# Channels in fours of neighbours: a new order of the model dimension through a two-layer transformer step, with 16 KB runs of expert weights

## The reference

```
aff = softmax(h @ w_router)                  # 640 x 16
gsel, idx = top_k(aff.T, C)                  # C = 64 latent + 16 context tokens per expert
xs = h[idx]                                  # 80 rows of 1024 channels
hid = silu(xs @ w_gate[e]) * (xs @ w_up[e])  # both weights 1024 x 1024
y += scatter(hid @ w_down[e] * gsel, idx)    # 1024 x 1024
```

## Time and profile before

| | us |
|---|---|
| three runs: median (lowest to highest) | 1780.83 (1779.23 to 1781.92) |
| profiled execution: its own time | 1777.96 |
| its span | 1776.2 |
| TensorE matmul busy / weight load busy | 1626.3 / 1275.9 |
| VectorE / ScalarE / GpSimd busy | 815.0 / 581.9 / 393.5 |

### The profile page before, as it was taken

How to read it: one execution, slowest core, us unless ns; L and a number is a source line. 1 busy time by engine, 2 the same in 40 slices (tenths; PEclk the granted TensorE clock), 3 DMA queues, 4 the chain that set the end, 5 groups by cost and what they waited for, 6 DMA issues and landing times.

```text
span 1776.2 us, 71059 instructions
## 1 busy us (share of the span) xinstructions
PE 1626.3 (92%) x27949; PEld 1275.9 (72%) x27949; DVE 815.0 (46%) x2574; ACT 581.9 (33%) x2311; POOL 393.5 (22%) x2167
## 2 busy tenths in 40 slices
PE   6999989988999999998869999999889998999994
PEld 3554457447999989988745454764489998998884
DVE  2199867153323333232344996843623232333233
ACT  2200157335545432221130002753445544121211
POOL 2100000002343424342310000000124333343332
PEclk9999999999999999999979999999999999999997
DMA  9446740238999999999963412321599999999993
GB/s 342 143 163 245 256 177 1 107 115 308 397 409 410 409 410 410 409 410 410 403 223 136 171 60 74 141 95 36 225 383 409 410 410 409 409 410 410 409 410 143
DMA packets 146646, 502.07 MB, mean 283 GB/s; under 512 B 6211, under 2 KB 6628, under 8 KB 146566
## 3 DMA queue, kind: packets, MB, share of 16 engines
q1 hardware_dynamic: 142276, 488.96, 70.8%
q0 software_dynamic: 3264, 10.88, 1.9%
q10 hardware_dynamic: 1026, 1.25, 0.2%
HBM read 494.76 MB, written 6.31 MB: 282 GB/s over the span
## 4 chain that ended last, share of the span: by engine, by line
PE 63%; DMA 25%; DVE 7%; ACT 2%; issue 2%; DVEq 0%; POOL 0%; POOLq 0%; ACTq 0%; SPq 0%
PE ps L957 18%; PE ps L702 15%; DMA weight_ring<-in_w_down_dram 11%; PE ps L974 9%; DMA weight_ring<-in_w_up_dram 8%; PE ps L840 7%; DMA weight_ring<-in_w_gate_dram 5%; PE ps L736 4%; PE ps L581 2%; DVE neg_m L1559 2%; PE ps L784 1%; PE ps L646 1%; ACT weight_ring L1151 1%; DMA qk<-in_x_sample_dram 1%; PE ps L894 1%
## 5 line engine op out<-in xcount | busy, mean ns | idle before, releaser
L957 PE MATMUL ps<-v_sb,weight_ring 128*64 128x80 f32 x16384 | 583.1, 233 | 29.5 <-DMA weight_ring<-in_w_gate_dram 14.4
L957 PEld LDWEIGHTS ps<-v_sb,weight_ring 128*64 128x64 f32 x16384 | 571.2, 137 | 41.2 <-DMA weight_ring<-in_w_gate_dram 18.2
L974 PE MATMUL ps<-v_sb,weight_ring 128*64 128x80 f32 x8192 | 295.0, 233 | 34.4 <-DVE v_sb L1720 21.6
L974 PEld LDWEIGHTS ps<-v_sb,weight_ring 128*64 128x64 f32 x8192 | 286.7, 137 | 42.7 <-DVE v_sb L1720 26.8
L702 PE MATMUL ps<-mix,weight_ring 128*128 128x128 f32 (+1 forms) x976 | 271.3, 439 | 2.1 <-ACT mix L1061 1.2
L1254 ACT ACTIVATE v_sb<-mix 128x8 f32 x1520 | 183.0, 204 | 228.8 <-PE ps L957 144.5
L1746 DVE TENSOR_TENSOR qk<-qk,v_sb 128x8 f32 x1520 | 210.9, 193 | 98.4 <-issue 95.8
L1880 POOL COPY v_sb<-mix 128x8 f32 x1040 | 145.4, 200 | 459.7 <-PE ps L957 396.0
L1893 POOL TENSOR_TENSOR qk<-qk,v_sb 128x8 f32 x1040 | 201.0, 237 | 178.1 <-DVE v_sb L1735 173.9
L702 PEld LDWEIGHTS ps<-mix,weight_ring 128*128 128x128 f32 x976 | 148.0, 194 | 123.2 <-issue 120.3
L1471 DVE SCALAR_TENSOR_TENSOR weight_ring<-u_gate,conv_cols,weight_ring 128x655 f32<-128x655 f32 x240 | 195.3, 893 | 0.0
(11 more groups left out here) (201 smaller groups left out, 1265.8 us busy)
## 6 DMA issues: line engine op xcount, KB each, us to landing
weight_ring<-in_w_down_dram SPq DMA_DIRECT2D x64, 2048.0 KB, 22.3
weight_ring<-in_w_gate_dram SPq DMA_DIRECT2D x48, 2048.0 KB, 19.5
weight_ring<-in_w_up_dram SPq DMA_DIRECT2D x48, 2048.0 KB, 23.0
weight_ring<-in_w_mod_dram SPq DMA_DIRECT2D x24, 2048.0 KB, 8.4
weight_ring<-in_w_in_dram SPq DMA_DIRECT2D x10, 2048.0 KB, 8.9
spare<-in_w_gate_dram SPq DMA_DIRECT2D x32, 512.0 KB, 10.7
weight_ring<-in_w_out_dram SPq DMA_DIRECT2D x4, 2048.0 KB, 9.5
rope_sb<-in_w_gate_dram SPq DMA_DIRECT2D x16, 512.0 KB, 11.5
```

The source lines that it names most:

```text
L957: last = nc.tensor.matmul(ps[c * HALF:(c + 1) * HALF, 2 * (i % 2) + f // BLK, f % BLK * CAP:(f % BLK + 1) * CAP], w[:, kk, o:o + HALF], pi ...
L974: last = nc.tensor.matmul(ps[c * HALF:(c + 1) * HALF, 4 + d // BLK, d % BLK * CAP:(d % BLK + 1) * CAP], w[:, kk, o:o + HALF], hid[:, k, :] ...
```

## The change

The channel order of the residual stream, and the hidden order in an expert, becomes: channel 512b + 4p + j lies on partition p, in chunk 4b + j (RUN = 4). `run_rows` reads a weight in that order, and the four rows that one partition needs of half a matrix are neighbours in memory. `in_run` is the matching slice of 128 (or 64) columns with a step of 4 elements.

1. `expert_unit`: one contiguous run of 16 KB per partition where four of 4 KB were. A relay piece remains 4 KB per partition.
2. The stationary slices in `gate_up` and `down` have a step of 4 elements (16 bytes).
3. `transpose_x`, `x2_transposes` and `modulation_cols` read with that step; `transpose_back` and the gate transposes write PSUM with it.
4. `proj_unit` issues four DMAs of 512 KB where it issued one of 2 MB (2 KB rows as before); `load_router` issues four.
5. The bias and gain rows are loaded as 512-wide rows and transposed with four strided slices per layer, beside one for the rest.
6. In units 0 and 1 TensorE goes through kk outermost and signals (`pieces_used`) after each of the first three quarters. ScalarE copies piece j as soon as quarter j was used, and the last when the unit was.

```diff
+RUN = 4
+        pieces_used = [signal(f"pieces_used{r}", (RELAY - 1) * EXPERTS) for r in range(RELAYS)]
+        def run_rows(w):
+            return w.rearrange("(b p j) n -> p b j n", p=P, j=RUN)
+        def in_run(k, p0=0, n=P):
+            first = k // RUN * RUN * P + k % RUN + RUN * p0
+            return slice(first, first + RUN * (n - 1) + 1, RUN)
...
+                for j in range(RUN):
+                    sp.dma_start(dst[:, :, j, :], src[:, :, j, :]).then_inc(proj_loaded[i % 2].sem, 16)
...
-                return w[l, e].rearrange("(k p) n -> p k n", p=P)[:, half * 4:half * 4 + 4, :]
+                return run_rows(w[l, e])[:, half:half + 1]
...
-                sp.dma_start(relay[r][j], expert_src(l, e, r)[:, j, :]).then_inc(relay_loaded[r].sem, 16)
+                sp.dma_start(relay[r][j], expert_rows(l, e, r)[:, j // RUN, j % RUN, :]).then_inc(relay_loaded[r].sem, 16)
...
-                sp.dma_start(ring[:, UNIT_SLOTS[l][i], :].rearrange("p (k n) -> p k n", k=KD // 2), expert_src(l, e, i))\
-                  .then_inc(expert_loaded[i].sem, 16)
+                sp.dma_start(ring[:, UNIT_SLOTS[l][i], :].rearrange("p (b n) -> p b n", b=1),
+                             expert_rows(l, e, i).rearrange("p b j n -> p b (j n)")).then_inc(expert_loaded[i].sem, 16)
...
-                    last = nc.tensor.transpose(ps[:, 2 * (t % 3) + k // 4, tokens(k % 4)], x2_t[:, k, tokens(t)], ident[:])
+                    last = nc.tensor.transpose(ps[:, 2 * (t % 3) + k // 4, in_run(k % 4)], x2_t[:, k, tokens(t)], ident[:])
...
-                                               x_all[:, t, tokens(k)], ident[:])
+                                               x_all[:, t, in_run(k)], ident[:])
...
+                        order = [(f, kk) for f in range(KD) for kk in range(KD // 2)]
+                        if i < RELAYS:
+                            order.sort(key=lambda at: at[1])
+                        for f, kk in order:
...
-                                        w[:, kk, o:o + HALF], picked_t[:, k, :],
+                                    w[:, kk, in_run(f, c * HALF, HALF)], picked_t[:, k, :],
...
+                            if i < RELAYS and f == KD - 1 and kk < RELAY - 1:
+                                last.then_inc(pieces_used[i].sem, 1)
...
                 def relay_copy(e, r):
-                    act.wait_ge(*expert_used.at(l, (e - 1) * 6 + r + 1))
                     act.wait_ge(*relay_loaded[r].at(l, e * RELAY))
-                    w = ring[:, UNIT_SLOTS[l][r], :].rearrange("p (j n) -> p j n", j=RELAY)
                     for j in range(RELAY - 1):
+                        act.wait_ge(*pieces_used[r].at(l, (e - 1) * (RELAY - 1) + j + 1))
                         nc.scalar.activation(w[:, j, :], relay[r][j], ACT.Copy).then_inc(relay_copied[r].sem, 1)
+                    act.wait_ge(*expert_used.at(l, (e - 1) * 6 + r + 1))
```

More of the change, by code:

```diff
@@ L165, in build @@
         conv_rows = free_slots[0:TAPS * CH, P:P + DEPTH * P].rearrange("p (l n) -> p l n", l=DEPTH)
-        par_rows = free_slots[0:C_ALL, 3 * P:3 * P + DEPTH * P].rearrange("p (l n) -> p l n", l=DEPTH)
+        chan_rows = free_slots[0:C_CB // RUN, 3 * P:3 * P + DEPTH * RUN * P].rearrange("p (l n) -> p l n", l=DEPTH)
+        par_rows = free_slots[0:C_ALL - C_CB, 12 * P:12 * P + DEPTH * P].rearrange("p (l n) -> p l n", l=DEPTH)
         past_k = x_norm[:, 0:DEPTH * BANK].rearrange("p (l n) -> p l n", l=DEPTH)
@@ L218, in build @@
         past_copied = signal("past_copied")
-        proj_loaded = [signal(f"proj_loaded{b}", 3 - b, 16) for b in range(2)]
+        proj_loaded = [signal(f"proj_loaded{b}", 3 - b, 16 * RUN) for b in range(2)]
         mod_loaded = [signal(f"mod_loaded{s}", unit=16) for s in range(SLOTS)]
@@ L293, in build @@
         h2_hi_ready = signal("h2_hi_ready", TILES)
-        router_loaded = signal("router_loaded", 1, 16)
+        router_loaded = signal("router_loaded", 1, 16 * RUN)
         strips_done = signal("strips_done", TILES)
@@ L416, in proj_unit @@
             def proj_unit(l, i):
-                sp.dma_start(ring[:, PROJ_SLOTS[l][i % 2], :].rearrange("p (k n) -> p k n", k=KD),
-                             rows8(w_in[l])[:, :, PROJ_ORDER[i] * BANK:(PROJ_ORDER[i] + 1) * BANK])\
-                  .then_inc(proj_loaded[i % 2].sem, 16)
+                dst = ring[:, PROJ_SLOTS[l][i % 2], :].rearrange("p (b j n) -> p b j n", j=RUN, n=BANK)
+                src = run_rows(w_in[l])[:, :, :, PROJ_ORDER[i] * BANK:(PROJ_ORDER[i] + 1) * BANK]
+                for j in range(RUN):
+                    sp.dma_start(dst[:, :, j, :], src[:, :, j, :]).then_inc(proj_loaded[i % 2].sem, 16)
             def mod_unit(l, u):
@@ L429, in out_unit, with expert_rows @@
                              rows8(w_out[l])[:, half * 4:half * 4 + 4, :]).then_inc(out_loaded[half].sem, 16)
-            def expert_src(l, e, i):
+            def expert_rows(l, e, i):
                 w, half = (w_gate, w_up)[i % 2] if i < 4 else w_down, i // 2 if i < 4 else i - 4
-                return w[l, e].rearrange("(k p) n -> p k n", p=P)[:, half * 4:half * 4 + 4, :]
+                return run_rows(w[l, e])[:, half:half + 1]
             def relay_piece(l, e, r, j):
-                sp.dma_start(relay[r][j], expert_src(l, e, r)[:, j, :]).then_inc(relay_loaded[r].sem, 16)
+                sp.dma_start(relay[r][j], expert_rows(l, e, r)[:, j // RUN, j % RUN, :]).then_inc(relay_loaded[r].sem, 16)
             def expert_unit(l, e, i):
-                sp.dma_start(ring[:, UNIT_SLOTS[l][i], :].rearrange("p (k n) -> p k n", k=KD // 2), expert_src(l, e, i))\
-                  .then_inc(expert_loaded[i].sem, 16)
+                sp.dma_start(ring[:, UNIT_SLOTS[l][i], :].rearrange("p (b n) -> p b n", b=1),
+                             expert_rows(l, e, i).rearrange("p b j n -> p b (j n)")).then_inc(expert_loaded[i].sem, 16)
             sp.dma_start(cond_rows[0:KD, :], c_ctx.rearrange("(k p) -> k p", p=P)).then_inc(cond_loaded.sem, 16)
@@ L545, in _ @@
                 o = PAR_COL + l * C_ALL
-                last = nc.tensor.transpose(ps[:, 7, o:o + C_ALL], par_rows[:, l, :], ident[0:C_ALL, 0:C_ALL])
+                for j in range(RUN):
+                    nc.tensor.transpose(ps[:, 7, o + j:o + C_CB - RUN + j + 1:RUN], chan_rows[:, l, in_run(j)],
+                                        ident[0:C_CB // RUN, 0:C_CB // RUN])
+                last = nc.tensor.transpose(ps[:, 7, o + C_CB:o + C_ALL], par_rows[:, l, :],
+                                           ident[0:C_ALL - C_CB, 0:C_ALL - C_CB])
             last.then_inc(setup_transposed.sem, 1)
@@ L590, in modulation_cols @@
                     col = MOD_COLS * (mod_region(l, group) * BLK + b)
-                    last = nc.tensor.matmul(ps[:, 7, col:col + MOD_COLS], mod_rows[:, tokens(b)], pair_sum,
+                    last = nc.tensor.matmul(ps[:, 7, col:col + MOD_COLS], mod_rows[:, in_run(b)], pair_sum,
                                             start=True, stop=True)
@@ L852, in x2_transposes @@
                     for k in range(KD):
-                        last = nc.tensor.transpose(ps[:, 4 + k // 4, tokens(k % 4)], x_tile[:, i % 2, tokens(k)], ident[:])
+                        last = nc.tensor.transpose(ps[:, 4 + k // 4, tokens(k % 4)], x_tile[:, i % 2, in_run(k)], ident[:])
                     last.then_inc(x2_transposed.sem, 1)
@@ L900, in _ @@
                         g = mod[:, l, 2 * KD + k, v:v + 1].to_broadcast([P, P])
-                        last = nc.tensor.transpose(ps[:, 2 + 2 * v + k // 4, tokens(k % 4)], g, ident[:])
+                        last = nc.tensor.transpose(ps[:, 2 + 2 * v + k // 4, in_run(k % 4)], g, ident[:])
                 last.then_inc(gates_transposed.sem, 1)
@@ L951, in gate_up @@
                         w = ring[:, UNIT_SLOTS[l][i], :].rearrange("p (k n) -> p k n", k=KD // 2)
[L952 to L959, removed]
-                                        w[:, kk, o:o + HALF], picked_t[:, k, :],
-                                        start=(k == 0 and f % BLK == 0), stop=(k == KD - 1 and f % BLK == BLK - 1))
+                        order = [(f, kk) for f in range(KD) for kk in range(KD // 2)]
+                        if i < RELAYS:
+                            order.sort(key=lambda at: at[1])
+                        for f, kk in order:
+                            k = (i // 2) * (KD // 2) + kk
+                            for c in range(2):
+                                last = nc.tensor.matmul(
+                                    ps[c * HALF:(c + 1) * HALF, 2 * (i % 2) + f // BLK,
+                                       f % BLK * CAP:(f % BLK + 1) * CAP],
+                                    w[:, kk, in_run(f, c * HALF, HALF)], picked_t[:, k, :],
+                                    start=(k == 0 and f % BLK == 0), stop=(k == KD - 1 and f % BLK == BLK - 1))
+                            if i < RELAYS and f == KD - 1 and kk < RELAY - 1:
```

(27 more changed lines are left out.)

## The result

The changed kernel takes 2349.2 us (median of 4 runs, 2348.29 to 2350.07) against 1780.0 (four runs, one more than in the table before): 1.3198 times as long, 95% interval 1.3175 to 1.3221. The forecast of 1751 us was wrong, and so was the size of the rival that named the cause (A, about 2150 us).

What follows compares the result with a forecast made beforehand. It took both expert stages as bound by the DMA rate. Longer runs win 34.0 us, strided transposes cost 4, the rest 0: 30 us less, 1777.96 to 1748, median 1751; 8-in-10 range 1737 to 1835.

Steps and rivals of the forecast that it cites:

- A: Rival: strided weight loads set the expert stages' pace; about 2150 us, light form near 1825; chance 0.25 (0.17 heavy, 0.08 light).
- What bounds the kernel: Both expert stages, 939 us together, are DMA-rate bound: 30.7 us per expert against 27.6 us of TensorE.
- part 1: Expert weight DMAs: 16 KB runs flow at 429 GB/s instead of 410, winning 17.0 us per layer, 34.0 in two.
- the signs: Expert stages if right: 425 to 430 GB/s, gate-and-up block 17.9 us, w_down's last unit 17 us earlier, first relay copy 3.
- the sum: Whole kernel: 34.0 - 4 = 30 us less, profiled execution 1777.96 to 1748, median 1751.
- part 4: Strided transposes, PSUM writes and strided x reads: 0 if free, 13 to 16 us if doubled; 4 us taken for all.
- Part 2: Quarters in units 0 and 1: win up to 3 us and new loss up to 3 us per layer; 0 taken.
- Part 3: Expert stationary operand at a 16-byte step: no cost taken, called a guess; upper end 53 ns per load.
- The threshold of 1.3 times: Expert weight loads could take 1.3 times as long per column (34.9/26.6) before setting TensorE's pace.
- The sign that I gave: Back-transposes: if they last 200 ns and more apiece, the cost of strided transposes was put too low.
- Part 5: Small edits: setup transposes 0, proj_unit's extra DMA issues 0 (at worst 2 us), router loads 0.

Runs made afterwards that it cites:

- e6: Changed kernel with gate, up and down stationary slices as 64 neighbouring columns again, a second time for its profile: 1752.2 us, ratio 0.9851.
- e1: Changed kernel with gate, up and down stationary slices as 64 neighbouring columns again, all else kept: 1752.2 us, ratio 0.9838 to the kernel before.
- e4: Kernel before with only the quarters (row chunks outermost in units 0 and 1, a signal after each of three quarters): 1777.1 us, ratio 0.9980.
- e7: Changed kernel with pairs (RUN = 2, 8 KB runs) and without the quarters, relay copies waiting for the whole unit: 1763.1 us, ratio 0.9911.
- e2: Kernel before with only the gate, up and down stationary slices at a step of 4 elements (16 bytes): 2345.1 us, ratio 1.3175.
- e5: Kernel before with stationary steps 3 and 12 for gate_up of layers 0 and 1, 8 and 2 for down: 2171.0 us, one execution.

## Why the prediction was wrong, point by point

**What bounds the kernel, and part 1: right.** Runs of 16 KB flow at 429 GB/s, runs of 8 KB at 422, as the line through two points had it. e6 is the forecast kernel without its strided expert loads, and its stages are 34.2 us shorter (34.0 forecast), the quarters' part in that included. Its first relay copy also comes 3.2 us earlier after the start of the stage, and its blocks last 17.9 us, as the signs had it. That it took 1752.2 us, next to the 1751 forecast, is in part luck: it gained 27 us on its kernel before and e1 28, where the sum had 30, because the time outside the stages grew by more than the 4 us of part 4.

**Part 2, the quarters at 0: mis-sized.** They gave 3.3 us on the kernel before (ratio 0.9968 to 0.9991). Both halves of the argument show in e4, the copy 3.2 us earlier and the next unit's issue 1.7 us later. Whether a faster DMA loses some of the gain again, as the step had it, is not settled (e7).

**Part 3 is the step that failed.** "I take no cost": the loads took 217 ns. The argument was that three lengths of load at 0.83 ns per column show the pace of the load path, with room behind it. Those rows all had neighbouring columns and could not speak on a step. The bounds failed too. I set the upper end at twice the time per column, 53 ns per load, by round number and not by a row; it is 2.5 times (0.83 + 1.25 = 2.08 ns). The way from there to the time was sound. Two loads side by side at 64 x 2.08 ns make 66.6 ns per load, where 60.1 was measured, and at step 3 the same working gives 45.5 against 43.7. With 60.1 ns in it, rival A would have come to 768 x 60.1 = 46 us per expert and some 2320 us, without the short waits between the blocks. The threshold of 1.3 times was not tested closely: step 3, at 1.7 times, is above it and slows TensorE, and no run lies between. So the failure is one price without a row, and the chance of 0.25 for a rival that no measured row spoke against.

**Part 4 at 4 us: near in sum, by luck.** Outside the expert stages the span grew from 837.2 to 842.5 us (845.2 in e6; from 838.4 to 840.5 in e2, e4 and e5, which have none of part 4, so some 3 us of it are scatter). The transposes that the 4 us were for show no cost from their step on PSUM. What grew is a group that part 4 had not named, the strided loads of `modulation_cols` (line 607 after, 591 before; 325 ns for 128 columns instead of 191), twice the time of each on the chain before the first projection:

```profile
28.09 2.02 PE ps L607 x8
...
48.69 1.66 PE ps L607 x8
```

where the chain before had 1.04 and 0.81 us. All seven of these groups stand on the chain and add 6.1 us in all. Groups by line in the changed kernel:

```profile
L632 PE MATMUL ps<-ident,qk 128*128 128x128 f32 x80 | 16.3, 389 | 15.6 <-DVE qk L1768 13.6 <-DVE mix L1802 2.0
...
L607 PE MATMUL ps<-strip_sum,x_tile 128*128 128x8 f32 x56 | 12.8, 355 | 0.8 <-ACT x_tile L1034 0.8
...
L917 PE MATMUL ps<-ident,mod 128*128 128x128 f32 x32 | 3.8, 273 | 0.0
```

The gate transposes, which write PSUM with the step, kept 273 ns, so no doubling there. `transpose_back` went from 13.2 to 16.3 us busy, but not by its step: in e2, where it has none, its matmuls last 376 ns on average, in e6, where it has it, 346 (329 before, 389 after). The sign that I gave, 200 ns and more apiece, could not tell anything: on the chain before they already took 206 (3.50 us for 17).

**Part 5:** x arrives as before (TensorE's first transpose of it at 14.42 against 14.41 us), and no cost of it shows beyond the scatter named above.

## What to carry to other kernels

Before a layout makes an inner access strided on an engine with little slack, price that access by an experiment, or carry its cost in the forecast; a row of unit stride says nothing on it. Here the longer runs should have stopped at the length that still leaves two float32 columns per 16 bytes for TensorE: pairs (8 KB runs) keep 19 of the 28 us that fours give when their loads cost nothing (e1, whose results are other numbers). And where two resources stand at 27.6 and 30.7 us per step, a gain on one is capped by the small reserve of the other, while a loss on the other is not.

## What the runs showed of the hardware

- A float32 stationary load of 64 columns takes 137 to 139 ns at steps of 4 or 8 bytes, 175 at 12, 217 at 16, 218 at 32 and 236 at 48. Loads of 128 columns in `modulation_cols` take 191, 196 and 325 ns at 4, 8 and 16 bytes.
- The loads of `transpose_x` take 142 ns with neighbouring columns, and 209 and 212 ns at steps of 8 and 16 bytes (medians).
- Runs of 2, 4, 8 and 16 KB flow at 387, 410, 422 and 429 GB/s. A fixed 9.6 ns per packet, worked out from the first two, meets the other two within 1 GB/s, and a run of 16 KB moves as one packet.
- A PSUM write with a step of 16 bytes did not lengthen the gate transposes (272.5 before, 272.7 ns after).
